# Combination weights folded into the FF values by slot, and expert rows added into the residual rows by accumulating DMA transfers

## The reference

```python
p_in = jax.nn.softmax(top_vals, axis=-1) * p_grp          # two weights per token
...
a = jnp.einsum('td,edf->tef', ht, wg)
b = jnp.einsum('td,edf->tef', ht, wu)
return jnp.einsum('tef,efd->td', jax.nn.silu(a) * b * c[:, :, None], wd)
...
x = x + hier_moe(h, ...)
return rms_norm(x, g_final)
```

## Time and profile before

| | us |
|---|---|
| median of 3 runs (736.08 to 736.93) | 736.88 |
| the profiled execution | 735.27 |
| its span, first to last instruction | 733.5 |
| PE busy | 569.4 |
| DVE busy | 349.3 |
| ACT busy | 259.4 |
| POOL busy | 248.9 |

### The profile page before, as it was taken

One profiled execution on the slowest core, in us unless ns is written; L12 is line 12 of the kernel. 1 busy time (PEld: TensorE's weight loads), 2 busy tenths in 40 slices (PEclk: granted clock), 3 DMA queues, 4 the chain that ended last, 5 costly groups with the idle time before them and its releaser, 6 DMA issues.

```text
span 733.5 us, 12088 instructions
## 1 busy us (share of the span) xinstructions
PE 569.4 (78%) x4249; PEld 378.2 (52%) x4250; DVE 349.3 (48%) x729; ACT 259.4 (35%) x443; POOL 248.9 (34%) x413
## 2 busy tenths in 40 slices
PE   3899999936989897989999519874599888597910
PEld 2677788624656564667787504432244444244400
DVE  4339999987886863478614441210012111021136
ACT  6344433302345644575332202331123332132312
POOL 5333344311212211135561034442124535133424
PEclk9999999975989998999999759997789999699965
DMA  8224443220122003302425999999997999996053
GB/s 277 61 61 133 153 116 89 84 57 0 58 58 58 1 1 114 114 9 107 143 69 207 381 408 404 408 409 409 409 409 312 364 407 407 408 410 243 24 206 147
DMA packets 58810, 149.19 MB, mean 203 GB/s; under 512 B 8660, under 2 KB 25044, under 8 KB 58782
## 3 DMA queue, kind: packets, MB, share of 16 engines
q1 hardware_dynamic: 53438, 139.89, 50.9%
q0 software_dynamic: 5200, 8.41, 3.1%
q10 hardware_dynamic: 144, 0.52, 0.2%
HBM read 145.37 MB, written 12.08 MB: 215 GB/s over the span
## 4 chain that ended last, share of the span: by engine, by line
PE 41%; DVE 29%; SPq 12%; DMA 8%; issue 5%; ACT 3%; POOL 1%; DVEq 1%; ACTq 0%; POOLq 0%
PE bank L631 18%; PE bank L852 10%; SPq L399 9%; DVE bank L1195 8%; DMA region<-in_w_e_up 5%; PE bank L869 5%; DVE bm L1173 4%; DVE m L1172 4%; DVE conv_buf L1164 2%; SPq L409 2%; PE bank L829 2%; PE bank L703 1%; PE bank L734 1%; DVE kT L1429 1%; PE bank L800 1%
## 5 line engine op out<-in xcount | busy, mean ns | idle before, releaser
L514 POOL TENSOR_TENSOR w_part<-region,w_part 128x1024 fp32r<-128x1024 f32 (+1 forms) x52 | 110.0, 2116 | 243.8 <-ACT w_part L903 243.8
L631 PE MATMUL bank<-h_hi,w_part 128*128 128x512 f32 (+1 forms) x528 | 171.9, 400 | 3.2 <-DVE h_lo L1122 1.7
L852 PE MATMUL bank<-region,kT 128*32 128x256 f32 x1536 | 99.9, 418 | 32.1 <-DMA region<-in_w_e_up 28.6
L631 PEld LDWEIGHTS bank<-h_hi,w_part 128*128 128x128 f32 (+1 forms) x528 | 99.7, 189 | 33.2 <-issue 7.1
L1443 DVE TENSOR_TENSOR mask_b<-mask_b,bank 128x128 f32<-128x128 f32 x30 | 8.6, 288 | 207.5 <-ACT mask_b L1081 207.5
L631 PE MATMUL bank<-h_lo,w_part 128*128 128x512 f32 (+1 forms) x264 | 104.3, 395 | 0.0
L852 PEld LDWEIGHTS bank<-region,kT 128*32 128x32 f32 x1536 | 58.5, 120 | 80.8 <-issue 60.0
L1195 DVE SCALAR_TENSOR_TENSOR bank<-glu,cv,bank 128x512 f32<-128x512 f32 x116 | 87.6, 755 | 19.0 <-DVE bank L1195 14.0
L903 ACT ACTIVATE w_part<-region 128x1024 fp32r<-128x1024 f32 (+1 forms) x52 | 48.1, 924 | 105.7 <-PE bank L631 105.7
L531 POOL TENSOR_TENSOR carrier<-mhalf 128x1 f32<-128x1 f32 x184 | 32.9, 196 | 145.0 <-ACT qT L1085 134.8
L631 PEld LDWEIGHTS bank<-h_lo,w_part 128*128 128x128 f32 (+1 forms) x264 | 49.9, 189 | 10.7 <-issue 0.2
(11 more groups left out here) (237 smaller groups left out, 801.0 us busy)
## 6 DMA issues: line engine op xcount, KB each, us to landing
region<-in_w_e_down SPq DMA_DIRECT2D x22, 1024.0 KB, 16.3
region<-in_w_e_gate SPq DMA_DIRECT2D x44, 512.0 KB, 13.4
region<-in_w_e_up SPq DMA_DIRECT2D x44, 512.0 KB, 13.8
region<-in_w_in SPq DMA_DIRECT2D x16, 1024.0 KB, 6.0
gates<-in_w_e_gate SPq DMA_DIRECT2D x20, 512.0 KB, 14.7
gates<-in_w_e_up SPq DMA_DIRECT2D x20, 512.0 KB, 15.0
conv_buf<-in_w_e_down SPq DMA_DIRECT2D x10, 1024.0 KB
region<-in_w_out SPq DMA_DIRECT2D x2, 2048.0 KB, 7.8
```

What stands on the lines that cost most here:

```text
L514: g.tensor_tensor(unit_part(u, 1), unit_raw(u), unit_part(u, 0).bitcast(F32), ALU.subtract)\
L631: last = mm(out_, a_parts[p], b_parts[q], start=start and x_ == 0, stop=stop and x_ == 2)
L852: last = mm(bank[0][32 * c:32 * c + 32, 0:FF], xTs[:, k, at_:at_ + 32], w_gu[slot][:, e, :, half, k, j * P:(j + 1) * P], start=(half == 0 ...
```

## The change

Three parts. (1) Once `wts` is known, DVE makes a float32 copy of `ohlo`, multiplies `ohhi` by the weights, and PE multiplies the two (32 small products), which gives `slot_w`: the weight of each slot, by tile. (2) In the loop `hid` is made by one instruction that also multiplies by the tile's column of `slot_w`; its place comes from the loop's register. (3) Behind the loop nothing is loaded to `yrow`. SP signals `rows_in`, and POOL issues eight transfers that add rows of `expert_rows` into `xr`: first those of choice 0 for the four blocks, then those of choice 1, each behind the completed one of the same block. The scaling at the end is whole rows on DVE for every block.

```diff
             dve: routing
+            v.tensor_copy(ohlo_f, ohlo)
             link(v.tensor_tensor(wts[:, 1, :], wts[:, 0, :], gs[:, 8, :], ALU.mult))
+            v.tensor_tensor(ohhi, ohhi, spread(wts[:, :, :].rearrange("p c b -> p (c b)"), 2, 2 * MAXT), ALU.mult)\
+                .then_inc(S["ohw_ready"], 1)
+            dve.wait_ge(S["sw_mm"], 1)
+            v.tensor_copy(slot_w[:], bank[5][:, 0:MAXT]).then_inc(S["sw_ready"], 1)
+            dve.wait_ge(S["sw_ready"], 1)
...
+            pe.wait_ge(S["ohw_ready"], 1)
+            for cc in range(2 * TB):
+                for c in range(4):
+                    last = mm(bank[5][32 * c:32 * c + 32, 0:MAXT], ohlo_f[:, cc, :],
+                              ohhi[:, cc, c // 2 * MAXT:(c // 2 + 1) * MAXT], start=(cc == 0), stop=(cc == 2 * TB - 1))
+            last.then_inc(S["sw_mm"], 1)
...
-                v.tensor_tensor(hid, sil, bank[0][:, P:2 * P], ALU.mult).then_inc(S["hid_ready"], 1)
+                v.scalar_tensor_tensor(hid, sil, slot_w[:, bass.ds(t, 1)], bank[0][:, P:2 * P], ALU.mult, ALU.mult)\
+                    .then_inc(S["hid_ready"], 1)
...
             sp: behind the waits for the scatters
-            for b in range(TB):
-                for c in range(2):
-                    sp.dma_start(yrow[:, 2 * ((b + 2) % TB) + c, :], y_dram[c * T + b * P:c * T + (b + 1) * P, :])\
-                        .then_inc(ld_y[b], 16)
+            sp.sem_inc(S["rows_in"], 1)
...
             pool: behind its loop
+            pool.wait_ge(S["rows_in"], 1)
+            for c in range(2):
+                for b in range(TB):
+                    if c:
+                        pool.wait_ge(add_y[0][b], 16)
+                    g.dma_start(xr[:, b, :], y_dram[c * T + b * P:c * T + (b + 1) * P, :], accum_op=ALU.add)\
+                        .then_inc(add_y[c][b], 16)
...
             act
-                act.wait_ge(S["y_add"], 2 * b + 2)
+                act.wait_ge(add_y[1][b], 16)
...
             dve: the end, in place of the adds of L1454 and the half scalings of L1464, L1093, L597
+            dve.wait_ge(ld_gbc, 32)
+            for b in range(TB):
+                mean_square(2, b)
+                dve.wait_ge(S["rstd_ready"], 2 * TB + b + 1)
+                v.scalar_tensor_tensor(xr[:, b, :], xr[:, b, :], rs[:, 2, b:b + 1], g_final_bc, ALU.mult, ALU.mult)\
+                    .then_inc(S["o_ready"], 1)
```

More of the change, by code:

```diff
@@ L150, in build @@
         gflat = gates[:, :, :].rearrange("p k n -> p (k n)")
-        yrow = r1[:, 0:8192].rearrange("p (u n) -> p u n", u=8)
         conv_buf = sb("conv_buf", [P, 2 * CC, T])
@@ L241, in build @@
         ohhi = gluf[:, cut[0] - 768:cut[0]].rearrange("p (c n) -> p c n", c=2 * TB)
+        ohlo_f = mask[:, 128:384].rearrange("p (c n) -> p c n", c=2 * TB)
         ohlo = mask[:, 0:128].bitcast(BF16).rearrange("p (c n) -> p c n", c=2 * TB)
@@ L253, in build @@
         wts = sb("wts", [P, 2, TB])
+        slot_w = sb("slot_w", [P, MAXT])
         ld_x = [sem(f"ld_x{b}") for b in range(TB)]
@@ L273, in build @@
         scattered = [sem(f"scattered{u}") for u in range(RING)]
-        ld_y = [sem(f"ld_y{b}") for b in range(TB)]
+        add_y = [[sem(f"add_y{c}_{b}") for b in range(TB)] for c in range(2)]
         st_out = sem("st_out")
@@ L282, in build @@
             rt_mm exp_in exp_out m_ready rank_mm oh_ready tab_mm tab_ready gu_half gu_mm silu_g hid_ready
-            hidT_mm hidT_ev y_mm yev_a xg_mm xtev_a xtev_v idx_copy y_add o_scaled o_half o_ready dve_chain pool_chain
+            hidT_mm hidT_ev y_mm yev_a xg_mm xtev_a xtev_v idx_copy rows_in ohw_ready sw_mm sw_ready o_ready dve_chain pool_chain
             ys_free rows_ready xg_ready sidx_copy""".split()
@@ L451, in _ @@
                 sp.wait_ge(scattered[n], ((tiles + (RING - 1 - n)) // RING) * 16)
-            for b in range(TB):
-                for c in range(2):
-                    sp.dma_start(yrow[:, 2 * ((b + 2) % TB) + c, :], y_dram[c * T + b * P:c * T + (b + 1) * P, :])\
-                        .then_inc(ld_y[b], 16)
+            sp.sem_inc(S["rows_in"], 1)
             for b in range(TB):
                 sp.wait_ge(S["o_ready"], b + 1)
-                if b < TB - 1:
-                    sp.wait_ge(S["o_half"], b + 1)
                 sp.dma_start(out[0, b * P:(b + 1) * P, :], xr[:, b, :]).then_inc(st_out, 16)
@@ L593, in _ @@
                     .then_inc(S["rstd_ready"], 1)
[L594 to L598, removed]
         @block.tensor
```

## The result

The changed kernel takes 743.02 us (median of 4 runs, 742.77 to 743.79) against 736.90 for the kernel before (736.08 to 738.12): a ratio of 1.0083, 95% interval 1.0066 to 1.0101. It is 6.1 us slower in the medians. The two profiled executions stand 7.7 us apart, 742.99 against 735.27, with spans of 741.2 and 733.5. A second set of runs of the same changed kernel gave 1.0075 (1.0051 to 1.0098).

What follows compares the result with a forecast made beforehand. The weight stream was taken to pace the expert loop, except a dip and behind the last load. The new start and adds put the end at 740.2, `hid` +1.0: 741.2 against 733.5, +7.7 on 736.88: 744.6 us, range 735 to 757.

Steps and rivals of the forecast that it cites:

- the store 1.3: At the end, block 0's scaled rows are stored on the DMA engines beside the adds: 1.29 us more.
- the last steps: After the last block's rows are complete, square, mean, power and scaling run without overlap: 3.5 us.
- Part 4, two reads an add: At the end, each 512 KB accumulating transfer costs two passes, 2.58 us; eight take 20.6 us. Chance 0.42.
- The rival at 2.1 us: Adds at the end: two source reads at a higher engine rate, +3.9 us in all, 740.8 us; chance 0.2.
- that of three passes (3.87): Adds at the end: three passes or a waited-for read, 3.87 us a transfer, +19.4, 756.3 us; chance 0.18.
- Part 3, POOL's way out of its loop: After the loop, POOL's skipped tiles delay the first add's issue to 707.55, where SP's was 704.84: +2.7 us.
- Part 2: In the expert loop, `hid` with the slot's weight costs 0.12 us in eight turns on the path: +1.0 us.
- the product reads the same two tiles: At `hid` in the loop, the product itself costs nothing more; only the instruction on registers is new, 0.12 us.
- Part 1: Making the slot weights before the expert loop takes 5.2 us at most, hidden: 0, upper end 1 us.
- What hides it is the first gather: Before the first tile, DVE is free until 436.68, so the slot weights' work, until 435.3, costs 0.
- a gather slowed by DVE beside it: At the first gather, DVE's work could delay it and remove the cover, by 1 us say.
- Nothing until 529.67 would move: In the early expert loop, a later first release of weights would be absorbed by the backlog: 0 us.

Runs made afterwards that it cites:

- the short loop: The changed kernel with POOL's loop bounded by the number of tiles rounded up to four instead of 48: 741.18 us, ratio 1.0046 to the kernel before.
- the fixed column: The changed kernel with the first column of `slot_w` for every tile, so no place from a register: 742.12 us, ratio 1.0057 to the kernel before.
- the weight at `ys`: The changed kernel with the weight as scale of ACT's copy to `ys`, DVE's product as before: 743.93 us, ratio 1.0085 to the kernel before.
- parts 1 and 2 alone: The changed kernel with the old end (SP's loads, DVE's adds, factor 1.0 for `wts`): 737.14 us against 737.11 for the kernel before, ratio 0.9997.
- part 3 alone: The changed kernel without slot weights, `hid` as before, expert rows added unweighted by the new end: 741.85 us, ratio 1.0063 to the kernel before.
- the slot weights behind the gather: The changed kernel with DVE waiting for POOL's first gather instruction before making slot weights: 742.36 us, ratio 1.0073 to the kernel before.
- part 1 alone: The changed kernel with `hid` and the end of before, slot weights made but unused: 738.75 us, ratio 1.0012 to the kernel before.
- the kernel that adds first: The changed kernel, weight in ACT's copy, short POOL loop; POOL adds choice 0 at once, DVE adds loaded choice 1: 740.26 us, ratio 1.0034.

## Why the prediction was right, and where its sizes were off

- **The forecast** was 744.6 us, and 743.0 was measured. The forecast +7.7 for the profiled execution is what the two profiles show, with a predicted span of 741.2 and a measured one of 741.2. That it fits to the tenth is partly chance: three terms were too large (the store 1.3, the transfers' duration 8 x 0.07 = 0.6, the last steps 0.2), and four too small (the last scatter 0.9, the start of the adds 0.4, the lead-in to their data 0.3, the last store 0.4). The last scatter's share is itself luck, as the last point of this section shows. The median came out 1.6 lower, because the changed kernel's profiled execution lies at its median while that of before lies 1.6 under it. The step from one to the other was the error here.
- **Part 4, two reads an add.** Right: 2.51 us a transfer where 2.58 was taken. As the edit to plain copies shows, it is the addition, not the queue or the order. The rival at 2.1 us and that of three passes (3.87) fall. The trace agrees with the ratio in the Trainium skill (Collectives: The Full Stack, "The bandwidth ceiling: the fold count and why AG ≠ RS ≠ AR"), an adding transfer at half of a copy's rate: 0.524 MB / 2.51 us = 209 GB/s against 406. It doesn't agree with the estimate of 248 GB/s from that page's 31 GB/s an engine.
- **The path in part 4.** From first issue to the last block's rows it took 23.1 us (709.87 to 732.98); 24.65 was predicted (707.55 to 732.2). The missing 1.5 is the term for a store beside the adds, 1.29, and 0.6 from the shorter transfers, less 0.3. No add was pushed back: the stores were issued at 728.90 and the bytes stayed at the adds' rate until the adds were done. The last store and the end take 4.94 us instead of 4.53, but not because of the adds, for with plain copies in their place it is 4.94 too (734.9 less 729.96); what makes it isn't shown. The last block's steps took 3.3 (732.98 to 736.26), 3.5 predicted.
- **Part 3, POOL's way out of its loop.** Right: 2.7 predicted, 3.1 measured (6.02 less 2.91), and the short loop gives 2.8 back. It is the one cost of the change that a line removes.
- **Part 2.** The mechanism is right, the count of turns and the size off. Nine turns pay, not eight, for the pair has six tiles. A turn costs 0.16 us, not 0.12: the instruction on registers cost 0.10. The term that was mis-sized is "the product reads the same two tiles", costed at nothing: with the column as a third operand it takes 348 ns, not 289. The traces bear this out one by one. From the end of that pair's first product to the issue of the load it takes 32.73 to 32.75 us in the seven profiles whose product on DVE is as before, 33.52 to 33.54 in the six with the new product, and 33.05 with the fixed column. From the end of the product behind the last load, where that took over 5 us, to the last scatter it takes 25.39 in the three profiles with the turn of before and 26.02 to 26.03 in four with the new one (25.51 to 25.52 with the weight at `ys`). That makes 0.80 + 0.64 = 1.4 us. The medians don't confirm it: parts 1 and 2 alone show +0.0, and the edit that moves the weight to ACT gains none of it.
- **Part 1.** "What hides it is the first gather" failed as a reason: the gather itself is delayed, by 1.2 to 1.5 us. That is the case which the prediction named, a gather slowed by DVE beside it, with a price of up to 1 us. The first product stands at 442.68, not near the 439.5 that the prediction named as its test; 1.6 of that is the later start of the tables, the rest the gather. "Nothing until 529.67 would move" doesn't quite hold, since the stream sags by a tenth to a quarter for some 6 us. From the tables' start to the pair of six tiles it is 103.4 us on average over the ten profiles with a delayed gather (102.95 to 104.01); over the four without (two of before, part 3 alone, the slot weights behind the gather) it is 102.8 (102.59 to 102.93). So some 0.6 us in the traces, which the medians can't confirm (1.0012, 0.9996 to 1.0029, for part 1 alone).
- **Luck, and what stays open.** In the profile after, the last scatter is 1.9 us late. In the order of time that is: the tables +1.56, before anything of the change had run; from them to the pair of six tiles +1.08; its first product -0.90; the five turns +0.80; the stream up to the last load +0.12; the product behind that load -1.69; the last turns +0.95. The gifts of PE's clock, the two products, and the late tables belong to single executions (see the last section), and they happen to cancel most of each other. By the traces parts 1 and 2 cost 0.6 + 1.4 = 2.0 us; by the medians 0 to 0.8 from one pair of kernels and 0.9 to 1.5 from the other. Which is right isn't settled. The total shows the same gap: 6.1 and 5.5 us in the two sets of runs, where the traces come to 2.0 + 5.8 = 7.8.

## What to carry to other kernels

A DMA transfer that adds into its destination moved at half the rate of a plain copy: it pays only where its bytes are few or the path has room for twice their time. Taking the adds off DVE was worth something here: with plain copies in their place the stretch from the first transfer's issue to DVE's last end is 19.3 us (710.68 to 729.96), where it was 24.1 before. But the later start took 3.1 of these 4.8 us, and the addition put 7.1 back on (26.4). Ask also what the new issuer is doing at that moment: a queue that must first run through a loop's skipped turns starts late, and an engine that was free before may be the reason why nobody noticed.

## What the hardware showed that was not expected

- **A gather lands later when DVE works while POOL issues it.** 8.0 to 8.3 us from issue to the rows' first use instead of 6.8, with a cast (0.33 us) and a product of 128x768 (0.96 us) beside the issue, and an issue of 1.29 us either way. The Trainium skill (SBUF — State Buffer, "SBUF: two separate sides") says that a copy on VectorE in a two-port mode keeps GpSimd from writing descriptors until it ends. The effect may be of that kind, but the delay is four times the cast's length, and no run shows the mode of the cast or which of the two instructions makes the delay.
- **Plain stores waited behind adding transfers that were already under way.** Issued at 728.90, the stores left the byte rate at 205 to 221 GB/s until 732, the adds kept their spacing, and then it was 383. It isn't a rule for all plain transfers: loads issued at the same time as the adds shared the engines with them (250 to 291 GB/s in the kernel that adds first).
- **A product on DVE with a column of factors** (128x128) takes 348 ns, without it 289, with a fixed column as with one from a register.
- **PE's clock behind a wait varies between executions.** The product behind the last load took 5.35 us before, after PE had idled for 3.9 us, and 3.66 in the changed kernel, after 2.2 us idle. A stretch within that product, before (the one of the changed kernel, 673.90 to 675.90, stands first among its stretches above):

```profile
673.20:675.20 2.00, 2.00 (x24) 1.27 (x20) 0.00 (x0) 0.00 (x0) 0.00 (x0) 0.50 0.12 43
```

  The granted clock is 0.50 (1.2 GHz) in the one and 1.00 (2.4 GHz) in the other, which is worth 1.7 us. The length of the wait alone doesn't decide it: in the second profile of the kernel before the product took 3.66 us behind 3.5 us idle, at a clock of 1.00, and in the kernel with the slot weights behind the gather 5.35 behind 2.5 us. So this isn't something that the change gave back.
- **Chance ahead of the change.** Over 14 profiles the routing tables began between 426.6 and 431.8 us, though no edit touches what runs before them. The profiled executions with the latest tables are also those which lie furthest above the median of their runs: 431.8 goes with 3.1 us above, 429.7 with 2.3. A landmark in one trace isn't worth more than that; differences between two landmarks of the same trace are, as the 32.73 and 33.53 above show.
